# A one-core hybrid layer: the final norm in two token pieces with plain transposes, and a 128-column copy ahead of a state write on ScalarE

## The reference, cut to what matters

```
x = x + 1/2 * SwiGLU_2(RMSNorm(x))
y = x * rsqrt(mean(x * x over the 1024 channels) + 1e-6) * norm_final_g      # per token
...
# branch B, for each of 4 groups of heads, chunk after chunk of the prompt:
state = decay * state + B^T (decayed inputs)       # the state after the last prompt chunk is an output
# then the same with the sampled tokens, each stream starting from its own old state
```

## Time and profile before

| what | value |
|---|---|
| median of 3 runs | 1894.99 us (1893.29 to 1895.34) |
| the profiled execution: its own time | 1895.05 us |
| its span in the trace | 1892.9 us |
| TensorE busy | 1862.7 us, 98% of the span |
| VectorE, ScalarE, GpSimd busy | 1111.5, 647.4, 137.7 us |

### The profile page before, as it was taken

How to read it: one execution, slowest core, us unless ns; L and a number is a source line. 1 busy time by engine, 2 the same in 40 slices (tenths; PEclk the granted TensorE clock), 3 DMA queues, 4 the chain that set the end, 5 groups by cost and what they waited for, 6 DMA issues and landing times.

```text
span 1892.9 us, 31449 instructions
## 1 busy us (share of the span) xinstructions
PE 1862.7 (98%) x12735; PEld 1817.8 (96%) x12735; DVE 1111.5 (59%) x1368; ACT 647.4 (34%) x842; POOL 137.7 (7%) x257
## 2 busy tenths in 40 slices
PE   8999999999999999999999999999999999999998
PEld 7999999999999999999989989998999999999998
DVE  6443443345777866767777877885855433442444
ACT  5221332123577742334244235233332211221223
POOL 3000000000012121111111101100200000000000
PEclk9999999999999999999999999999999999999999
DMA  5222222222422253354354335335622222222222
...
DMA packets 273342, 186.14 MB, mean 98 GB/s; under 512 B 7452, under 2 KB 260580, under 8 KB 273008
## 3 DMA queue, kind: packets, MB, share of 16 engines
...
...
## 4 chain that ended last, share of the span: by engine, by line
PE 88%; DVE 6%; ACT 3%; issue 2%; DMA 0%; ACTq 0%; DVEq 0%
PE pu L647 80%; PE pn L899 1%; PE pn L849 1%; DVE w_lo L1403 1%; PE pn L867 1%; PE pn L744 1%; PE pn L871 1%; PE pn L890 1%; PE pu L706 0%; DVE bc L1397 0%; DVE squares L1397 0%; PE pn L838 0%; PE pu L909 0%; PE pn L664 0%; DVE xc L1397 0%
## 5 line engine op out<-in xcount | busy, mean ns | idle before, releaser
L1403 DVE TENSOR_TENSOR w_lo<-w_raw,w_hi 128x1024 fp32r<-128x1024 f32 x240 | 296.5, 1235 | 460.2 <-ACT w_hi L985 458.7
L647 PE MATMUL pu<-act_hi,w_hi 128*128 128x320 f32 x1952 | 456.9, 315 | 6.7 <-DVE xc L1397 2.2
L647 PE MATMUL pu<-act_lo,w_hi 128*128 128x320 f32 x1952 | 447.2, 310 | 1.1 <-DVE act_lo L1446 1.0
L647 PE MATMUL pu<-act_hi,w_lo 128*128 128x320 f32 x1952 | 446.7, 310 | 0.0
L985 ACT ACTIVATE w_hi<-w_raw 128x1024 fp32r<-128x1024 f32 x240 | 253.5, 1056 | 520.8 <-PE pu L647 519.6
L647 PEld LDWEIGHTS pu<-act_hi,w_hi 128*128 128x128 f32 x1952 | 327.3, 189 | 21.3 <-issue 17.1
L647 PEld LDWEIGHTS pu<-act_lo,w_hi 128*128 128x128 f32 x1952 | 328.5, 189 | 2.4 <-DVE act_lo L1446 1.5
L647 PE MATMUL pu<-x_hi,w_hi 128*128 128x320 f32 x1440 | 329.3, 310 | 1.3 <-DVE ff_g L1459 1.3
L647 PEld LDWEIGHTS pu<-act_hi,w_lo 128*128 128x128 f32 x1952 | 328.7, 189 | 0.0
L647 PE MATMUL pu<-x_lo,w_hi 128*128 128x320 f32 x1440 | 328.5, 309 | 0.0
L647 PE MATMUL pu<-x_hi,w_lo 128*128 128x320 f32 x1440 | 328.4, 309 | 0.0
...
## 6 DMA issues: line engine op xcount, KB each, us to landing
...
```

Of the source, the lines that this page charges most:

```text
L647: ins = pe.matmul(dst[:, h, :], w[:, side, c, :], a[:, k, h * HALF:(h + 1) * HALF], start=(at == 0), stop=(at == n - 1))
L1403: dve.tensor_tensor(w_lo[:, side, :, :], w_raw[:, side, :, :], w_hi[:, side, :, :].bitcast(F32), ALU.subtract).then_inc(s["w_lo_done"], 1)
```

## The change

It makes two edits. At the end: ACT writes `x_gain`, a copy of each finished tile of `resid` times the gain; `to_rows` becomes 8 plain transposes of `x_gain`, and `g_fin` goes. The last unit computes its first 320 tokens wholly before the last 320 (`last_unit`), and the norm runs in two pieces, tokens 0 to 255 (tiles 0 and 1) and 256 to 639 (tiles 2 to 4), through `token_sums`, `token_var`, `token_root` and `token_scale`, the latter in 4 operations where it was 5. The last tile is scaled by ACT and DVE, half each, and sent in two DMAs. In the group end: ACT copies B of the fifth tile ahead of the prompt's state and its DMA, which were ahead of it. The diff, cut to what is spoken of:

```diff
-            g_fin = sb(sc, "g_fin", [P, KT, P])
             y_out = sb(sc, "y_out", [P, NT, D_MODEL])
             fin = sb(sc, "fin", [P, 8, NT])
+            x_gain = sb(sc, "x_gain", [P, KT, TOK])
...
-        fin_at = (pn[1], pu[O_FIN % 2], pu[(O_FIN + 1) % 2], pn[0], pn[1])
+        fin_at = (pn[1], pu[O_FIN % 2], pn[0], pu[(O_FIN - 1) % 2], pn[1])
+        fin_sums = pu[(O_FIN - 1) % 2][:, 0, HALF:HALF + NT]
...
-            for t in range(NT):
-                sp.wait_ge(s["y_v" if t % 2 else "y_a"], t // 2 + 1)
-                dst = y_prompt[0, t * P:(t + 1) * P, :] if t < NT - 1 else y_sample.rearrange("b l d -> (b l) d")
-                sp.dma_start(dst, y_out[:, t, :]).then_inc(s["y_dma"], 16)
-            sp.wait_ge(s["y_dma"], 16 * NT)
+            for t, name, n in ((0, "y_a", 1), (1, "y_a", 2), (2, "y_v", 1), (3, "y_a", 3)):
+                sp.wait_ge(s[name], n)
+                sp.dma_start(y_prompt[0, t * P:(t + 1) * P, :], y_out[:, t, :]).then_inc(s["y_dma"], 16)
+            for b, name, n in ((0, "y_a", 4), (1, "y_v", 2)):
+                sp.wait_ge(s[name], n)
+                sp.dma_start(y_sample.rearrange("b l d -> (b l) d")[:, b * 512:(b + 1) * 512],
+                             y_out[:, NT - 1, b * 512:(b + 1) * 512]).then_inc(s["y_dma"], 16)
+            sp.wait_ge(s["y_dma"], 16 * (NT + 1))
...
+                    last = u == U_FFN2 and gi == len(FFN_GROUPS) - 1
+                    with pe.Fori(0, KT // 2 - (1 if last else 0)) as i:
                         for k in range(2):
                             unit(ud + k, od + k, 2, 2, i, mid_hi, mid_lo, n, ready=hidden if k == 0 else None)
+                    if last:
+                        unit(ud + KT - 2, od + KT - 2, 0, 0, 0, mid_hi, mid_lo, n)
+                        last_unit(ud + KT - 1, od + KT - 1, mid_hi, mid_lo, n)
+            def token_sums(part):
+                pe.wait_ge(s["fin_add"], part + 1)
+                for t in ((0, 1), (2, 3, 4))[part]:
+                    ins = pe.matmul(fin_sums[:, t:t + 1], rvar[:, t * P:(t + 1) * P], ones[:, 0:1], start=True, stop=True)
+                ins.then_inc(s["fin_sum"], 1)
+            def last_unit(u, o, hi, lo, nk):
+                pe.wait_ge(s["w_lo_done"], u + 1)
+                open_out(o)
+                for h in range(2):
+                    for k in range(nk):
+                        if h == 1 and k == nk - 1:
+                            token_sums(0)
+                        for w, a in ((w_hi, hi), (w_lo, hi), (w_hi, lo)):
+                            ins = pe.matmul(out(o)[:, h, :], w[:, u % 2, k, :], a[:, k, h * HALF:(h + 1) * HALF],
+                                            start=(k == 0 and w is w_hi and a is hi), stop=(k == nk - 1 and a is lo))
+                    ins.then_inc(s["out_ready" if h else "fin_half"], 1)
...
-            def to_rows(t, k):
-                return pe.matmul(fin_at[t][:, k // 4, (k % 4) * P:(k % 4 + 1) * P], resid[:, k, t * P:(t + 1) * P], g_fin[:, k, :],
-                                 start=True, stop=True)
-
-            pe.wait_ge(s["gfin"], 1)
+            def to_rows(t):
+                for k in range(KT):
+                    ins = pe.transpose(fin_at[t][:, k // 4, (k % 4) * P:(k % 4 + 1) * P], x_gain[:, k, t * P:(t + 1) * P], ident[:, :])
+                ins.then_inc(s["out_ready"], 1)
+            pe.wait_ge(s["fin_g"], KT)
+            to_rows(0)
             pe.wait_ge(s["out_free"], O_FIN - 1)
-            for t in range(2):
-                for k in range(KT - 1):
-                    to_rows(t, k)
+            to_rows(1)
+            token_sums(1)
+            pe.wait_ge(s["fin_g"], KT + 1)
+            to_rows(2)
             pe.wait_ge(s["out_free"], O_FIN)
-            for t in range(2):
-                to_rows(t, KT - 1).then_inc(s["out_ready"], 1)
-            for k in range(KT // 2):
-                to_rows(2, k)
-            pe.wait_ge(s["sq_added"], SQ_FIN + KT)
-            for t in range(NT):
-                ins = pe.matmul(pn[0][:, 0, t:t + 1], rvar[:, t * P:(t + 1) * P], ones[:, 0:1], start=True, stop=True)
-            ins.then_inc(s["sq_summed"], 1)
-            for k in range(KT // 2, KT):
-                ins = to_rows(2, k)
-            ins.then_inc(s["out_ready"], 1)
-            pe.wait_ge(s["fin_v"], 1)
-            for k in range(KT):
-                ins = to_rows(3, k)
-            ins.then_inc(s["out_ready"], 1)
+            pe.wait_ge(s["fin_v"], 6)
+            to_rows(3)
             pe.wait_ge(s["y_a"], 1)
-            for k in range(KT):
-                ins = to_rows(4, k)
-            ins.then_inc(s["out_ready"], 1)
+            to_rows(4)
...
+                                if final:
+                                    act.activation(feature_tile(x_gain, i * 2 + k), feature_tile(resid, i * 2 + k), ACT.Copy,
+                                                   scale=v(i * 2 + (V_NFIN + k))).then_inc(s["fin_g"], 1)
+                                else:
                                     act.activation(feature_tile(x_hi, i * 2 + k), feature_tile(resid, i * 2 + k), ACT.Copy,
                                                    scale=v(i * 2 + (V_NMIX + k))).then_inc(s["xh_done"], 1)
                     if last:
                         act.activation(ln_col[:, :], eps_col[:, :], ACT.Sqrt).then_inc(s["ln_ready"], 1)
-                        for k in range(KT - 2, KT):
-                            act.wait_ge(s["out_free"], od + k + 1)
-                            square_tile(SQ_FIN + k, k % 2, resid[:, k, :])
+                        k = KT - 2
+                        act.wait_ge(s["out_free"], od + k + 1)
+                        square_tile(SQ_FIN + k, 0, resid[:, k, :])
+                        act.activation(x_gain[:, k, :], resid[:, k, :], ACT.Copy, scale=v(V_NFIN + k)).then_inc(s["fin_g"], 1)
+                        act.wait_ge(s["sq_added"], SQ_FIN + KT - 2)
+                        for h in range(2):
+                            part = slice(h * HALF, (h + 1) * HALF)
+                            if h == 0:
+                                act.wait_ge(s["fin_r"], 1)
+                            else:
+                                token_root(0)
+                                act.wait_ge(s["out_free"], O_FIN)
+                            act.activation(squares[:, 1, part], resid[:, KT - 1, part], ACT.Square).then_inc(s["fin_sq"], 1)
+                            act.activation(x_gain[:, KT - 1, part], resid[:, KT - 1, part], ACT.Copy,
+                                           scale=v(V_NFIN + KT - 1)).then_inc(s["fin_g"], 1)
+            def token_root(part):
+                cols = (slice(0, 2), slice(2, NT))[part]
+                act.wait_ge(s["fin_v"], 5 * part + 1)
+                act.activation(fin[:, 2, cols], fin[:, 1, cols], ACT.Sqrt).then_inc(s["fin_a"], 1)
...
+                    if t == NT - 1:
+                        act.wait_ge(s["hp_mm"], g + 1)
+                        act.activation(hp_rows[:, :, :].rearrange("p q n -> p (q n)"), pn[1][:, 1, :], ACT.Copy).then_inc(s["hp_cp"], 1)
+                        act.wait_ge(s["hp_cp"], g + 1)
+                        act.dma_start(hp_dst[:, g * PAIRS:(g + 1) * PAIRS, :], hp_rows[:, :, :]).then_inc(s["hp_out"], 16)
                     if t == NT - 1 and beside_last[0] == "gl":
                         fetch_branch(beside_last[1])
                     fill(held)
@@ -1286,11 +1330,6 @@
                         fill(beside[t] + behind[t][:-1])
                         decays(g, t + 1)
                         held = behind[t][-1:]
-                    if t == NT - 2:
-                        act.wait_ge(s["hp_mm"], g + 1)
-                        act.activation(hp_rows[:, :, :].rearrange("p q n -> p (q n)"), pn[1][:, 1, :], ACT.Copy).then_inc(s["hp_cp"], 1)
-                        act.wait_ge(s["hp_cp"], g + 1)
-                        act.dma_start(hp_dst[:, g * PAIRS:(g + 1) * PAIRS, :], hp_rows[:, :, :]).then_inc(s["hp_out"], 16)
...
-            act.wait_ge(s["tails_out"], 16 * TAIL_DMAS)
-            act.wait_ge(s["fin_v"], 1)
-            act.activation(fin[:, 2, :], fin[:, 1, :], ACT.Sqrt).then_inc(s["fin_a"], 1)
-            for t in range(0, NT, 2):
+            def rows_out(t, banks):
                 act.wait_ge(s["out_ready"], O_FIN + t + 1)
-                act.wait_ge(s["fin_v"], 6)
-                act.activation(y_out[:, t, :].rearrange("p (b c) -> p b c", b=2), fin_at[t][:, :, :], ACT.Copy,
+                act.wait_ge(s["fin_v"], 5 if t < 2 else 10)
+                act.activation(y_out[:, t, 0:banks * 512].rearrange("p (b c) -> p b c", b=banks), fin_at[t][:, 0:banks, :], ACT.Copy,
                                scale=fin[:, 5, t:t + 1]).then_inc(s["y_a"], 1)
+            rows_out(0, 2)
+            token_root(1)
+            rows_out(1, 2)
+            rows_out(3, 2)
+            rows_out(4, 1)
...
-                        for k in range(2):
```

(31 more changed lines are left out.)

18 lines of the change are left out of this document (5 added, 13 removed).

## The result

The changed kernel takes 1883.83 us (median of 5 runs, 1882.37 to 1884.39), the kernel before 1893.29 in the same comparison: ratio 0.995, with an interval from 0.9936 to 0.9965. The profiled execution took 1884.39 us, its span is 1882.6 for the 1892.9 of the earlier trace rows.

What follows compares the result with a forecast made beforehand. TensorE was taken as the bound (88% of the chain that ended last). Span 1892.9 - 4.8 (tail) - 2.3 (group ends) = 1885.8; with 2.15 over span, less 0.06, 1887.9 us; range 1886.2 to 1890.9.

Steps and rivals of the forecast that it cites:

- The tail: End of kernel: first output DMA 5.3 us earlier, a stream gap of 0.5 us, span 4.8 us shorter.
- The hole between tiles 0 and 1: Output stream: DMA engines idle 0.5 us because the second piece's root stands ahead of tile 1 on ACT.
- The weighted copies: Last units: ACT weights each finished tile, 0.82 us more per unit, fitting a hole of 1.3 us, costing nothing.
- rival (d): Last units: weighted copies on ACT delay the weight cuts, so the kernel is slower, 1899 us; chance 0.03.
- Rival (b): Tail: granted clock halves while TensorE runs only transposes, stream ends 1.4 us later, 1889.3 us; chance 0.09.
- Group 1: End of group 1: TensorE's wait of 0.77 us goes, since DVE gains more than that; 0.77 us won.
- group 2: End of group 2: `w_lo` starts 0.23 us ahead of `b_seq`; 1.7 of TensorE's 2.0 us wait saved.
- rival (a): Groups 1 and 2: `b_seq` still precedes `w_lo`, the lock eats the gain, tail alone gives 1890.6 us; chance 0.16.
- Group 0: End of group 0: ACT waits for TensorE's transposes, so no gain; one lock may cost 0.1 to 0.2 us.
- The base: Whole kernel: starting point of the sum, one profiled execution with span 1892.9 us, 0.06 over the median of 1894.99.
- The offset: Whole kernel: the execution takes 2.15 us more than its span, carried over to the changed kernel.
- theory B: From the experiments, not the prediction: the change itself takes away the falls of TensorE's granted clock.

Runs made afterwards that it cites:

- e5_best: Changed kernel with narrow products moved two input tiles, tile 1 scaled on DVE ahead of the second variance, tile 2 in halves: 1883.16 us, ratio 0.9953.
- c0_before: The kernel before, unchanged, run again: 1893.11 us, ratio 0.9996.
- e1_mid: The kernel before with only the group-end edit: 1888.81 us, ratio 0.9974.
- e9: The kernel before with the group-end edit and the narrow products moved two input tiles: 1888.83 us, ratio 0.9978.
- e7: The kernel before with only the narrow 16-column products moved two input tiles further from new_state(1): 1890.89 us, ratio 0.9989.
- e4: The changed kernel with the narrow 16-column products moved two input tiles further from new_state(1): 1883.75 us, ratio 0.9944.

## Why the prediction missed its range

The forecast lies 4.4 us above the mean of the changed kernel's 20 runs. The mechanism named for the tail and for groups 1 and 2 is right; what failed is the base that everything was taken from, the offset between span and time, group 0, and the falls of the clock, which the sum did not have.

**The tail, forecast -4.8, measured -4.63: right in size, with two errors that cancel in part.** The last unit is 0.46 us longer by the channel sums inside it, which did not wait; the first DMA leaves 5.83 - 0.46 = 5.37 us earlier (5.3 forecast). The hole between tiles 0 and 1 is there, at the place named, but of 0.3 us and not 0.5. The stream's end comes 0.4 us later than full DMA engines would have it, which the sum put at nothing (see e5_best). From the first DMA to the end it is 8.25 us before and 9.0 after, where the forecast's steps give 8.75. The half operations took 0.49 and 0.47 us. The weighted copies cost nothing (0.82 us each; ACT still idles 0.56 us for TensorE ahead of each of the last weight cuts), and rival (d) had nothing to stand on. Rival (b) did not come: the clock stayed at 1.00 through all transposes. The value of the transposes was right in the sum, though I had not seen that they halve TensorE's time for a tile.

**Group 1, forecast -0.77, measured -0.87; group 2, -1.7 and -1.90: right**, and rival (a) with its lock did not come. `w_lo` got in 0.24 us ahead of `b_seq`, forecast 0.23. The other half of the rule shows as well: `b_seq` ended 0.89 us behind that `w_lo`, while `squares`, with an operand from PSUM, ran beside it in its usual 0.81. The Trainium skill (SBUF — State Buffer, "SBUF: two separate sides") gives the lock to VectorE operations with two SBUF inputs, against a GpSimd operation that reads SBUF; the trace agrees on both.

**Group 0, forecast +0.1, measured -0.4: wrong.** The step that failed: "in group 0 ACT waited 0.48 us for TensorE's own transposes, and nothing is gained". The releaser named was TensorE, but what held ACT was its own DMA issue ahead of `b_tok`: in c0_before `b_tok` begins 0.73 us behind the start of the last transposes (783.82) and right behind the issue's end (784.51), in e1_mid 0.42 us behind them. So it comes 0.31 us earlier against TensorE's work, and the way to `gbuf` 0.1 us more: its start, 0.26 us earlier in the trace, is 0.43 us earlier against TensorE, whose row is 0.17 us later there. TensorE's wait of 0.43 us for `gbuf`, which the prediction did not have, is gone. The loss of 0.1 to 0.2 us by a lock did not come either: DVE's three convolution operations take 3.39 us in e1_mid and 3.50 in c0_before.

**The base, 2.3 us too high: wrong.** The step that failed: "the profiled execution took 2.15 us more than its span and lay 0.06 over the median of 1894.99". The sum starts from one execution, with the median of three as its confirmation. Over 110 runs the kernel before has a mean of 1892.7 us and stands between 1890.0 and 1896.6; the profiled execution had falls at 518 (of double length), 814 and 1286 us. The kernel's own lowest time is about what is left with one of these four units: 1895.05 less 3 x 1.55 is 1890.4. The prediction read the clock only in the tail; windows over the whole trace would have shown it.

**The offset, 0.35 us: wrong.** The same step carries the 2.15 us over to the changed kernel, which has 1.80.

**The falls, about 1 us: not in the forecast.** Then 1887.9 - 2.3 (base) - 0.7 (terms: 7.8 for 7.1) - 0.35 (offset) = 1884.5, and the mean of the changed kernel's 20 runs is 1883.5 (standard error 0.3). The 1.0 us left is, by estimate, two thirds of a fall fewer in an execution. The profiles bear the sum out: with 1.55 us taken off for each fall (the double one twice), 1886.7 and 1886.9 us are left of the spans of the kernel before (two profiles) and 1879.1 to 1879.5 of those of the changed kernel (four), so 7.5 us for the 7.8 of the terms. What is shown: the excess goes with the group-end edit (17 runs of it alone: 1888.3, so 4.4 us for 3.1 to 3.2 of waits; the tail alone, 7 runs: 4.4 for 4.6 and the 0.35), and there is none once the narrow products are moved (e9 against e7: 2.9 for 3.1; e4 against e7: 7.7 for 8.2). The profiles point the same way: with the narrow products in their old place, a fall at 812 to 814 us stands in 4 of 5 without the edit in group 0 and in 0 of 9 with it. But it is no clean removal, since with no fall at 814 one at 1126 often comes. What is not shown is how a wait that goes near 795 us keeps a fall away at 814. The parts of the edit by themselves did not show the excess (0.6 and 2.4 us for 0.4 and 2.7 of waits, each uncertain by 0.5). That stays open, and theory B is only half right.
